# A hybrid decoder layer on 8 cores: the pooling difference moves to GpSimd and is issued earlier, one constant load gets its own semaphore, and three small pieces change engine or place

## The reference

```
hn = rmsnorm(x, g_mix);  z = hn @ w_in            # columns: u 512, b 512, c 512, h 512, gp 1024, gc 1024
# pooling branch: 4 groups of 128 channels, trailing windows w = 2, 4, 8, 16
win  = sum of the last w rows of ext(u);  cnt = min(w, t + 1 + n_valid)
d    = win / cnt - u
pool = (d @ w_pool_group[g]) * pool_scale
# convolution branch
v = c * h;  conv = b * (w0*v[t-2] + w1*v[t-1] + w2*v[t])
x = x + (sigmoid(gp) * (pool @ w_pool_up) + sigmoid(gc) * (conv @ w_conv_out)) @ w_o
x = x + (silu(g) * u) @ w_ffn_out                 # g, u = rmsnorm(x, g_ffn) @ w_ffn_in
x = x + sigmoid(rmsnorm(x, g_ple) @ w_ple_gate) * (p @ w_ple)
y = rmsnorm(x, g_final)
```

## Time and profile before

| | us |
|---|---|
| median of 3 runs | 1147.48 |
| the three runs | 1244.39, 1124.69, 1147.48 |
| the profiled execution | 1123.71 |
| its span on the slowest core (core 0) | 1122.2 |
| spans of the 8 cores | 1113.1 to 1122.2 |
| granted TensorE clock, mean over a core's span | 0.958 to 0.968 |

### The profile page before, as it was taken

One profiled execution on the slowest core, in us unless ns is written; L12 is line 12 of the kernel. 1 busy time (PEld: TensorE's weight loads), 2 busy tenths in 40 slices (PEclk: granted clock), 3 DMA queues, 4 the chain that ended last, 5 costly groups with the idle time before them and its releaser, 6 DMA issues.

```text
span 1122.2 us, 15626 instructions; the slowest of 8 cores (1113.1 to 1122.2 us)
## 1 busy us (share of the span) xinstructions
PE 981.8 (87%) x5287; PEld 481.3 (43%) x5386; DVE 483.7 (43%) x625; ACT 295.8 (26%) x534; POOL 222.4 (20%) x220
## 2 busy tenths in 40 slices
PE   0347588989999999898999999999999999986994
PEld 0224244435444544454444444444444444443442
DVE  0352358553222222783272722632531441384555
ACT  0442131212222222332101011011011001385775
POOL 4001817002433342000101001001101000000553
PEclk9988889889999999998999999999999999998998
DMA  9652132227453356543334424424743500000243
GB/s 143 134 150 19 11 33 27 19 20 97 40 46 29 29 48 101 145 131 60 34 40 38 57 19 39 57 20 38 102 61 33 69 1 1 1 1 29 94 141 137
DMA packets 109230, 64.32 MB, mean 57 GB/s; under 512 B 94735, under 2 KB 96911, under 8 KB 109136
## 3 DMA queue, kind: packets, MB, share of 16 engines
q0 software_dynamic: 93280, 32.64, 28.1%
q1 hardware_dynamic: 10322, 30.09, 8.4%
q10 hardware_dynamic: 5550, 0.58, 0.6%
HBM read 86.66 MB, written 9.50 MB: 86 GB/s over the span
## 4 chain that ended last, share of the span: by engine, by line
PE 79%; issue 6%; DVE 5%; ACT 4%; DMA 3%; ACTq 2%; POOL 2%; DVEq 0%; POOLq 0%; SPq 0%
PE psum L93 79%; DVE t L93 5%; ACT t L93 3%; POOL t L93 2%; ACTq L121 2%; DMA t<-xp 1%; DMA t<-sconv 1%; ACT L93 0%; DMA t<-ppr 0%; DVEq L104 0%; ACTq L104 0%; POOLq L104 0%; SPq L120 0%; POOL t L121 0%; POOLq L120 0%
## 5 line engine op out<-in xcount | busy, mean ns | idle before, releaser
L93 PE MATMUL psum<-t,t 128*128 128x512 bf16 (+2 forms) x5287 | 981.8, 346 | 127.6 <-DVE t L93 48.9
L93 PEld LDWEIGHTS psum<-t,t 128*128 128x128 bf16 (+1 forms) x5386 | 481.3, 100 | 627.6 <-issue 165.7
L93 DVE TENSOR_TENSOR t<-psum,t 128x1024 f32<-128x1024 f32 (+6 forms) x421 | 369.4, 881 | 470.4 <-PE psum L93 427.3
L93 ACT ACTIVATE t<-psum 128x128 f32<-128x128 f32 (+5 forms) x263 | 144.8, 552 | 629.9 <-PE psum L93 597.2
L93 POOL TENSOR_TENSOR t<-t,t 128x512 bf16<-128x512 f32 (+2 forms) x57 | 83.7, 1474 | 297.2 <-DVE t L93 286.4
L93 ACT ACTIVATE t<-t 128x1 f32<-128x1 f32 (+4 forms) x145 | 89.4, 624 | 79.5 <-DVE t L93 54.6
L121 POOL DMA_DIRECT2D t<-w_ffn_in x44 | 38.9, 891 | 339.4 <-PE psum L93 339.4
L93 DVE SCALAR_TENSOR_TENSOR t<-t,t,t 128x512 f32<-128x512 f32 (+2 forms) x57 | 55.4, 983 | 21.1 <-ACT t L93 17.4
L121 POOL DMA_DIRECT2D t<-w_in x32 | 28.6, 903 | 143.7 <-PE psum L93 127.8
L93 POOL TENSOR_TENSOR t<-t 128x2062 f32<-128x2062 f32 (+7 forms) x20 | 47.3, 2365 | 7.4 <-DVE t L93 5.1
L93 ACT ACTIVATE t<-t,t 128x1024 bf16<-128x1024 f32 (+2 forms) x37 | 32.7, 883 | 60.8 <-DVE t L93 60.8
(11 more groups left out here) (10 smaller groups left out, 5.8 us busy)
## 6 DMA issues: line engine op xcount, KB each, us to landing
t<-xp SPq DMA_DIRECT2D x32, 512.0 KB, 4.2
t<-w_ffn_in POOLq DMA_DIRECT2D x44, 256.0 KB, 6.1
t<-w_in POOLq DMA_DIRECT2D x32, 256.0 KB, 8.0
yp<-t SPq DMA_DIRECT2D x16, 512.0 KB, 3.3
t<-w_ffn_out POOLq DMA_DIRECT2D x4, 1024.0 KB, 12.9
t<-w_o POOLq DMA_DIRECT2D x1, 2048.0 KB, 18.9
t<-w_ple_gate POOLq DMA_DIRECT2D x1, 2048.0 KB, 24.6
t<-ppr SPq DMA_DIRECT2D x16, 128.0 KB, 3.2
```

What stands on the lines that cost most here:

```text
L93: fn = (lambda eng, meth=meth, kw=kw: getattr(eng, meth)(**kw))
```

## The change

1. g_mix gets a resource and a semaphore of its own (`Rg0`, `dg0`), and the first norm's multiplication waits for that instead of `Rconst`.
2. In `s2_front` the transposes of the pooling history and their copy are issued after the five blocks instead of before them.
3. `s2_back_d` moves from VectorE (four instructions) to GpSimd (five): the window sum is multiplied in place by 1/w (`rcnt` entry 15, broadcast) over columns 31 on, by `rcnt` over the first 16 columns, and by 1/w in the sample part; then two subtractions write `dbuf`.
4. The read-out in `s2_gmm` moves from VectorE to ScalarE.
5. The order of the work becomes:

```diff
-    for i, gsrc in enumerate([g_mix, g_ffn, g_ple]):
+    Rg0 = Res(); Dg0 = em.newsem("dg0")
+    em.dma("act", gT[0][:, :], g_mix.rearrange("(c p) -> p c", p=128), Dg0, writes=[Rg0], allow_slow_non_contiguous=True)
+    for i, gsrc in [(1, g_ffn), (2, g_ple)]:
...
-            reads=[Rps[b], Rconst], writes=[Rh[t]])
+            reads=[Rps[b], (Rg0 if gidx == 0 else Rconst)], writes=[Rh[t]])
...
     def s2_back_d(g):
...
-        em.op("dve", "scalar_tensor_tensor", dict(out=dd[:, 0:SEQ], in0=win[:, 15:15 + SEQ], scalar=1.0 / w,
-                                                  in1=U[:, 15:15 + SEQ], op0=ALU.mult, op1=ALU.subtract),
+        rw = rcnt[:, g, 15:16]
+        em.op("pool", "tensor_tensor", dict(out=win[:, 31:15 + SEQ], in0=win[:, 31:15 + SEQ],
+                                            in1=rw.to_broadcast([128, SEQ - 16]), op=ALU.mult),
+              reads=[Rrcnt], writes=[rwin])
+        em.op("pool", "tensor_tensor", dict(out=win[:, 15:31], in0=win[:, 15:31], in1=rcnt[:, g, :], op=ALU.mult),
+              reads=[Rrcnt], writes=[rwin])
+        em.op("pool", "tensor_tensor", dict(out=us_view(win)[:, :, 15:23], in0=us_view(win)[:, :, 15:23],
+                                            in1=rw.unsqueeze(2).to_broadcast([128, 16, 8]), op=ALU.mult),
+              reads=[Rrcnt], writes=[rwin])
+        em.op("pool", "tensor_tensor", dict(out=dd[:, 0:SEQ], in0=win[:, 15:15 + SEQ], in1=U[:, 15:15 + SEQ], op=ALU.subtract),
               reads=[rwin, Ru[ui]], writes=[Rd[di]])
...
-            em.op("dve", "tensor_scalar", dict(out=pool_out[:, g, CB[tb]:CB[tb] + n], in0=psum[:, b, 0:n],
-                                               scalar1=pscale[:, g:g + 1], scalar2=None, op0=ALU.mult),
+            em.op("act", "activation", dict(out=pool_out[:, g, CB[tb]:CB[tb] + n], in_=psum[:, b, 0:n], func=AF.Copy,
+                                            scale=pscale[:, g:g + 1]),
...
-        em.op("act", "activation", dict(out=pbf[i][:, :], in_=pin[t % 4][:, :], func=AF.Copy), reads=[Rpin[t % 4]], writes=[Rpbf[i]])
+        em.op("pool", "tensor_tensor", dict(out=pbf[i][:, :], in0=pin[t % 4][:, :], in1=yst[0][:, 0:256], op=ALU.add),
+              reads=[Rpin[t % 4], Rz7], writes=[Rpbf[i]])
```

More of the change, by code:

```diff
@@ L557, in s2_front @@
         slot = load_w()
[L558 to L565, removed]
         for tb in range(5):
@@ L578, in s2_front @@
                       reads=[Rps[b]], writes=[Ru[ui]])
+        b = nb()
+        for hh in range(2):
+            em.op("pe", "transpose", dict(out=psum[:, b, hh * 120:(hh + 1) * 120],
+                                          in_=stp[hh][0:120, g * 128:(g + 1) * 128], identity=identf[0:120, 0:120]),
+                  reads=[Rconst, Ridentf], writes=[Rps[b]], sig=(hh == 1))
+        em.op("act", "activation", dict(out=us_view(U)[:, :, 0:15],
+                                        in_=psum[:, b, 0:240].rearrange("p (s r) -> p s r", r=15), func=AF.Copy),
+              reads=[Rps[b]], writes=[Ru[ui]])
         b = nb()
@@ L614, in s2_back_d @@
         dd = dbuf[di]
-        w = wins[g]
-        em.op("dve", "scalar_tensor_tensor", dict(out=dd[:, 0:SEQ], in0=win[:, 15:15 + SEQ], scalar=1.0 / w,
-                                                  in1=U[:, 15:15 + SEQ], op0=ALU.mult, op1=ALU.subtract),
+        rw = rcnt[:, g, 15:16]
[8 more added lines that the diff above has]
+        em.op("pool", "tensor_tensor", dict(out=dd[:, 0:SEQ], in0=win[:, 15:15 + SEQ], in1=U[:, 15:15 + SEQ], op=ALU.subtract),
               reads=[rwin, Ru[ui]], writes=[Rd[di]])
-        em.op("dve", "scalar_tensor_tensor", dict(out=dd[:, SEQ:NTOK].rearrange("p (s j) -> p s j", j=8),
-                                                  in0=us_view(win)[:, :, 15:23], scalar=1.0 / w,
-                                                  in1=us_view(U)[:, :, 15:23], op0=ALU.mult, op1=ALU.subtract),
+        em.op("pool", "tensor_tensor", dict(out=dd[:, SEQ:NTOK].rearrange("p (s j) -> p s j", j=8),
+                                            in0=us_view(win)[:, :, 15:23], in1=us_view(U)[:, :, 15:23], op=ALU.subtract),
               reads=[rwin, Ru[ui]], writes=[Rd[di]])
[L623 to L628, removed]
     def s2_gmm(g):
@@ L647, in build_nc @@
     s2_back_pool(1); s2_back_d(1)
-    s2_back_pool(2)
+    s2_gmm(0)
+    s2_back_pool(2); s2_back_d(2)
     Rv = [[Res() for _ in range(5)] for _ in range(2)]
@@ L731, in build_nc @@
         em.dma("sp", nps[s, 7:15, :], ustage[s * 8:(s + 1) * 8, 1, :], Dust, reads=[Rust], final=True)
-    s2_gmm(0)
-    s2_back_d(2)
-    s2_back_pool(3)
     s2_gmm(1)
+    s2_back_pool(3); s2_back_d(3)
     s3_chunk(1)
@@ L738, in build_nc @@
     s3_chunk(2)
-    s2_back_d(3)
     s2_gmm(3)
@@ L943, in s7_c @@
                 em.dma("sp", ytile(tt), x_res[:, tt, :], Dyo[tt % 4], reads=[Rx[tt]], final=True)
+    Rz7 = mk7(1)[0]
+    em.op("pool", "memset", dict(ap=yst[0][:, 0:256], constant=0.0), writes=[Rz7])
     s7_pin(0)
```

## The result

The change makes the kernel slower: the ratio to before is 1.0261, with a 95% interval of 1.0239 to 1.0284, some 29 us on 1124.9 (the median of ten runs of before). The profiled execution took 1154.3 us, its span on the slowest core, core 4, is 1152.8. The prediction said 1128.1 us in a range of 1110 to 1148, and gave 14% to a loss over 2%. It is wrong. The comparison leaves disturbed runs out; with them the median of the changed kernel is 1180.93 us.

What follows compares the result with a forecast made beforehand. TensorE bounds the kernel, busy 981.8 of 1122.2 us; only its idle 140 us can be had. Start -10.4 + 0.6, middle +13.2, stage 7 +1: +4.4 on 1123.71 gives 1128.1 us, range 1110 to 1148.

Steps and rivals of the forecast that it cites:

- Stage 7: Last stage, copy moved from ScalarE to GpSimd: a loss of 1 us, the pair of tiles at about 9.8 us.
- a loop of about 9.8 through it: Stage 7, pair of tiles: GpSimd's copy of some 0.7 us before each addition makes the period 9.8 instead of 9.74.
- The bounds of -4 and +6: Stage 7: from most of the 0.72 us wait of some 8 pairs coming free to 0.75 us more per pair.
- GpSimd bound: Rival, stage 7: GpSimd's copy and addition in line, 0.75 us a pair, 1133 us in all; chance 0.11.
- The start: Up to the first block of matmuls: a gain of 10.4 us, from 4.7 to 12.4; moved history transposes cost 0.6.
- I take 7 us: Start: x tile 4's load, issued near 26.8, takes 7 us and lands at 33.8, 2 us late.
- the rival that the backlog takes it: Rival, start: x tile 4 lands 7.7 us late behind the load backlog, 1134 us in all; chance 0.15.
- The middle: Pooling and convolution, paced by GpSimd's queue: a loss of 13.2 us, TensorE restarting 24.7 us later, part given back afterwards.
- my 5.4 us a block: Middle, chunk(1): VectorE's blocks come every 5.4 us against TensorE's 5.26, giving a 4.4 us stall before chunk(2).
- its bounds of +5 to +18: Middle: low with d at 8.8 us and no stall, high with d at 10.6 and 3 us more contention.
- three signs that I had named for being wrong: Middle and stage 7: no long TensorE idle, a d over 12 us, or stage 7's pair falling to 9.1 us.
- The dear broadcast: Rival, middle: GpSimd's broadcast multiplication takes 9 us instead of 4, +19, 1147 us in all; chance 0.12.

## Why the prediction was wrong

**Stage 7: this step failed most.** The prediction put the conversion on GpSimd at 0.7 us and worked out "a loop of about 9.8 through it, 0.1 per pair". The price is right where VectorE leaves GpSimd alone (3.04 less 2.35 for the addition), and 9.8 is what the conversion gives where it stands one tile earlier (9.88 measured). But I looked at the period of a pair, at the addition of the pair's second tile and at the conversion behind it, and took the first tile's addition as given by the loop of before. I left out that VectorE issues the copy of transposes k before product k-1, so that TensorE's own tile drives the addition for which its next tile waits: 5.6 us from tile to tile (1066.24 to 1071.83) and 6.2 in the second (to 1078.04), against 4.6 of work. I also put nothing down for GpSimd and VectorE holding each other up here, though I had priced that in the middle: the scalings went from 2.48 to 4.60 us, the conversion beside them from 0.74 to 1.72. The bounds of -4 and +6 were made from the same incomplete picture; 15 came. The rival named it ("GpSimd bound"), at 0.75 a pair; it was 2.06.

**The start: the mechanism was named, its size wasn't bounded.** ScalarE free at 22.8 was right for core 0 (22.34; on the others it was 20.6 to 28.2), tile 4's request at 26.8 too (26.29). The failing term is the landing, "I take 7 us" and at most 12.7: it was 14.1 on core 0. The worst of the first tiles was no upper bound, since these were issued before the weights and tile 4 behind eight of them. It was the wrong kind of term as well: the tile came when the backlog let it, near 40 us, so that asking earlier only made the wait longer. The gain was 3.3 us over the eight cores (4.0 and 5.5 in the ledger) instead of 10.4; the rival that the backlog takes it was true, and cost 5 to 7 us. The Trainium skill says that a DMA engine goes round the queues packet by packet (DMA: Bandwidth & Descriptors, "Queues, rings and completion order"). I had read from it that a load on SP's queue doesn't stand behind the weights on GpSimd's, and this case doesn't bear that reading out: with six of the eight weight loads held back the wait was gone.

**The middle: right in mechanism and place, short by 3 to 4 us.** d is 9.76 us where I had 10.1. Counted from the first block, TensorE restarts 24.3 us (core 0) and 26.0 (core 4) later than before, where I had 24.7 and 0.6 for the transposes; the wait ahead of it is 25.33 where I said about 27. The figure of the Trainium skill (GPSIMD Engine Reference, "Elementwise — side-by-side cycle accounting"), 4497 ns for 2048 columns, agrees with the subtraction (4506 ns) and not with the multiplication (3641 ns for 2032), for which my 4.0 was 0.4 too dear and the lower bound of 3.6 right. What was short is what comes back later: 8 us instead of 11.5. The waits behind chunk(1) are 2.40 + 4.58 instead of 4.4, since my 5.4 us a block came from beside pool(3) and the last taps stood behind d(3)'s subtraction, and TensorE's clock behind them was 0.74 for 12 us, some 3 us more that the sum had left out after this stall. The middle's +16.4 to +18.0, less the 0.6 of the transposes, lies within its bounds of +5 to +18.

**The sum.** With the terms as measured on core 0, -4.0 + 16.4 + 15.1 gives +27.5, near the 29 of the ratio. The three misses all went the same way, 6, 3 and 14 us. The range had room for the start and the middle both at their bad ends: with stage 7 at its bound of +6 the same sum is +18, 1142 us. It is stage 7 beyond its bound that led out of the range. None of the three signs that I had named for being wrong came up; a pair well above 9.8 was not among them. The dear broadcast, the rival on the slow side, didn't happen.

## What to carry to other kernels

When an operation moves to another engine's in-order list, write down for one tile who waits for whom through every list it touches, the neighbours' lists too; its place behind the previous tile's work can cost more than its own duration (1.0 us a tile here, beside 0.7 of its own), and one step earlier can cost almost nothing. Look for small instructions queued behind long ones (a 0.1 us memset was worth 2.8% of the changed kernel), and put what depends on nothing first. Before starting a load earlier, look at what the DMA engines do at that time: holding back the weights that aren't needed yet was worth more than the earlier start itself.

## What the runs showed of the hardware that I had not expected

- A 512 KB load of x behind eight weight loads took 14 us on core 0, against 4.1 on idle engines, though it was on another queue, and on all cores it came near 40 us whether asked for at 26 or at 32; with six of the eight held back, the tile's norm didn't wait at all.
- On GpSimd, multiplying 2032 columns by a broadcast column in place takes 3.6 us, as an addition of two shifted views of one tile, while a subtraction of two tiles takes 4.5 for 2048: the price goes by the operands. One addition of two shifted views, the last level of pool(3) over 2048 columns, took 4.8 in both kernels, which this doesn't explain.
- GpSimd and VectorE hold each other up on operands in SBUF: the pair of final scalings went from 2.48 to 4.60 us, addition and conversion from 3.04 to 4.01. Two taps of 128 columns went from 0.81 to 4.00 and ended only behind GpSimd's 4.5 us subtraction, so a short operation can wait for the whole of a long one. VectorE's products with an operand in PSUM didn't change: one beside GpSimd's addition in the run with the conversion one tile earlier (1086.34) took 1.22 us, as always.
- Issuing the ten constant loads, seven of them of 2 to 4 KB, held ScalarE's own queue for 20 to 28 us, depending on the core (first activation table load at 22.34 on core 0 and 28.23 on core 4 of the same execution), and for 17 to 21 us where six of the weight loads were held back.
